# Transferring the compression units past the split, waiting tile by tile in block 1's output, and moving a merge result's evacuation

## The reference

```python
def compress(t, pos_emb, w1, b1, w2):          # once for keys, once for values
    ...
    flat = jnp.moveaxis(blocks, 3, 2).reshape(b, -1, g, CMP_BLOCK * d)
    return jax.nn.gelu(flat @ w1 + b1) @ w2

# block 1
mixed = jnp.concatenate([y_lru, y_moba.astype(x.dtype), y_mem.astype(x.dtype)], axis=-1)
x = x + mixed @ w_out[l]

# block 2
g_conv, g_nsa, g_mem = jnp.split(jax.nn.sigmoid(merge_g), 3, axis=-1)
```

## Time and profile before

| | |
|---|---|
| timed runs | 1745.99, 1747.80, 1747.87 us; median 1747.8 |
| profiled execution | 1752.43 us, span 1750.5 us |
| granted TensorE clock, mean | 0.999 |
| TensorE busy | 1736.1 us (99%) |
| VectorE, ScalarE busy | 61%, 53% |
| moved | 328.51 MB, mean 188 GB/s |

### The profile page before, as it was taken

The page is one execution under the profiler, slowest core; times in us unless marked ns, Lnnn a source line. Parts: engine busy times, 40 slices in busy tenths (PEclk is TensorE's granted clock), DMA queues, the critical chain, the costliest instruction groups (busy, mean ns, idle before and its releaser), DMA issues.

```text
span 1750.5 us, 31143 instructions
## 1 busy us (share of the span) xinstructions
PE 1736.1 (99%) x12548; PEld 1593.0 (91%) x12548; DVE 1073.6 (61%) x1502; ACT 930.8 (53%) x1271; POOL 34.9 (2%) x60
## 2 busy tenths in 40 slices
PE   9999999999999999999999999999999999999998
PEld 9999988999999999988898999899999888989997
DVE  6555787655665566546677555755584557676555
ACT  6444577444454445576756444644464587664443
POOL 0000120000000000000000000000000000000000
PEclk9999999999999999999999999999999999999999
DMA  8655434655665555553355555655554543446552
GB/s 331 235 192 190 170 121 145 219 190 193 223 227 192 190 183 194 182 200 127 139 192 181 193 192 198 231 204 195 192 204 176 191 169 121 168 158 218 190 192 96
DMA packets 47551, 328.51 MB, mean 188 GB/s; under 512 B 5488, under 2 KB 5744, under 8 KB 9072
## 3 DMA queue, kind: packets, MB, share of 16 engines
q1 hardware_dynamic: 44640, 316.86, 50.4%
q10 hardware_dynamic: 2832, 10.54, 1.6%
HBM read 326.33 MB, written 1.05 MB: 187 GB/s over the span
## 4 chain that ended last, share of the span: by engine, by line
PE 94%; ACT 3%; DVE 1%; issue 1%; DMA 0%; POOL 0%; SPq 0%; DVEq 0%; POOLq 0%; ACTq 0%
PE work L1742 19%; PE work L1744 19%; PE work L1743 19%; PE acc L1744 8%; PE acc L1743 8%; PE acc L1742 8%; PE work L1982 4%; PE work L1851 3%; PE acc L2066 1%; PE acc L2048 1%; ACT prob L856 1%; PE acc L2058 1%; ACT hi L662 1%; DMA xT_raw<-xT 0%; PE work L1805 0%
## 5 line engine op out<-in xcount | busy, mean ns | idle before, releaser
L1161 DVE TENSOR_TENSOR lo<-raw,hi 128x2048 fp32r<-128x2048 f32 x271 | 620.3, 2291 | 323.0 <-ACT hi L662 322.8
L662 ACT ACTIVATE hi<-raw 128x2048 fp32r<-128x2048 f32 x271 | 518.7, 1915 | 380.9 <-PE work L1744 354.0
L1742 PE MATMUL work<-xT_hi,hi 128*128 128x256 f32 x2464 | 687.5, 279 | 3.0 <-ACT merge L846 2.5
L1744 PE MATMUL work<-xT_hi,lo 128*128 128x256 f32 x2464 | 683.0, 277 | 0.0
L1743 PE MATMUL work<-xT_lo,hi 128*128 128x256 f32 x2464 | 683.0, 277 | 0.0
L1742 PEld LDWEIGHTS work<-xT_hi,hi 128*128 128x128 f32 x2464 | 463.2, 188 | 12.4 <-issue 6.9
L1743 PEld LDWEIGHTS work<-xT_lo,hi 128*128 128x128 f32 x2464 | 463.8, 188 | 2.3
L1744 PEld LDWEIGHTS work<-xT_hi,lo 128*128 128x128 f32 x2464 | 464.4, 188 | 0.0
L1744 PE MATMUL acc<-hi,hT_lo 128*128 128x512 f32 x480 | 188.8, 393 | 0.0
L1743 PE MATMUL acc<-lo,hT_hi 128*128 128x512 f32 x480 | 188.4, 392 | 0.0
L1742 PE MATMUL acc<-hi,hT_hi 128*128 128x512 f32 x480 | 186.8, 389 | 0.0
(11 more groups left out here) (327 smaller groups left out, 2105.0 us busy)
## 6 DMA issues: line engine op xcount, KB each, us to landing
raw<-stream SPq DMA_DIRECT2D x297, 1024.0 KB, 4.8
mem_in<-mem ACTq DMA_DIRECT2D x3, 1024.0 KB, 5.0
post<-post ACTq DMA_DIRECT2D x6, 512.0 KB, 4.0
memT_raw<-mem2T ACTq DMA_DIRECT2D x2, 1024.0 KB, 7.1
xT_raw<-xT SPq DMA_DIRECT2D x2, 512.0 KB, 5.4
raw<-stream SPq DMA_DIRECT2D x2, 512.0 KB, 6.9
x<-x SPq DMA_DIRECT2D x2, 512.0 KB, 11.0
memT_raw<-mem1T ACTq DMA_DIRECT2D x1, 1024.0 KB, 11.4
```

The costliest lines, as they stand in the source:

```text
L662: nc.scalar.activation(dst, raw[:, s, :], ACT.Copy).then_inc(hi_ready, 1)
L1161: nc.vector.tensor_tensor(lo[:, s, :], raw[:, s, :], hi[:, s, :].bitcast(F32), ALU.subtract).then_inc(lo_ready, 1)
L1742: nc.tensor.matmul(dst, a_hi, b_hi, start=start, stop=False)
L1744: return nc.tensor.matmul(dst, a_lo, b_hi, start=False, stop=stop)
```

## The change

Three edits.

1. A compression unit is transferred by SP straight to its buffer of `whole` (`load_exact`). It waits till TensorE has used the unit three before it, which held that buffer. It has its own two semaphores, `exact_landed`, one for each half of a pair, and `landed` counts these units no more. ScalarE does nothing for it. VectorE counts it in `hi_ready` and `lo_ready` with two `memset`s that wait for nothing. TensorE waits on `exact_landed`. SP's order is: key unit 0, merge 1, key unit 1, value unit 0, value unit 1, then merge 2 and on.
2. `mixed_ready` waits for two attention tiles at kt 4, three at kt 6, four at kt 7; before, for three at kt 4 and four at kt 7.
3. For merge 0 and 1, ScalarE evacuates the result ahead of the split of the merge unit that comes next, where before it did so behind it.

```diff
     def landed(self, n):
-        return 16 * (self.unit(n) // RING + 1)
+        exact = sum(u <= self.unit(n) and u % RING == self.slot(n) for u in EXACT_UNITS)
+        return 16 * (self.unit(n) // RING + 1 - exact)
...
+            def load_exact(n, half):
+
+                sp.wait_ge(unit_used, n - RING + 1)
+                sp.dma_start(whole[:, n % RING, :], stream[n]).then_inc(exact_landed[half], 16)
...
                 base = B1_UNITS + layer * L_UNITS
-                turns = (base + 1 - at) // RING
-                load_turns(at, at + RING * turns)
-                at += RING * turns
+                at = load_turns(at, base + 1)
                 sp.dma_start(params[:, 0:LP_N], l_params[layer]).then_inc(params_loaded, 16)
-            turns = (UNITS - at) // RING
-            load_turns(at, at + RING * turns)
-            for n in range(at + RING * turns, UNITS):
+                first, end = base + L_EXACT[0], base + L_EXACT[-1] + 1
+                at = load_turns(at, first)
+                for n in range(at, first):
+                    load(n)
+                load_exact(first, 0)
+                load(first + 2)
+                load_exact(first + 1, 1)
+                load_exact(first + 3, 0)
+                load_exact(first + 4, 1)
+                at = end
+            at = load_turns(at, UNITS)
+            for n in range(at, UNITS):
                 load(n)
...
             def split_high(sec, n, trip=0):
 
                 s = sec.slot(n)
+                if exact(sec, n):
+                    return
                 wait(act, unit_used, sec.unit(n - RING + 1) + trip * RING)
                 act.wait_ge(landed[s], sec.landed(n) + trip * 16)
-                dst = (whole if exact(sec, n) else hi)[:, s, :]
-                nc.scalar.activation(dst, raw[:, s, :], ACT.Copy).then_inc(hi_ready, 1)
+                nc.scalar.activation(hi[:, s, :], raw[:, s, :], ACT.Copy).then_inc(hi_ready, 1)
...
                     if kind == "merge":
                         split_high(sec, L_MERGE[k] + 2)
+                        merge_out(k)
                         if k < 2:
                             split_high(sec, L_CMP[k] + 2)
-                        merge_out(k)
...
             def split_low(sec, n, trip=0):
                 s = sec.slot(n)
+                if exact(sec, n):
+                    k = 2 * (len(L_EXACT) * sec.layer + L_EXACT.index(n))
+                    nc.vector.memset(passed[:, k:k + 1], 0.0).then_inc(hi_ready, 1)
+                    nc.vector.memset(passed[:, k + 1:k + 2], 0.0).then_inc(lo_ready, 1)
+                    return
                 dve.wait_ge(hi_ready, sec.unit(n + 1) + trip * RING)
-                if exact(sec, n):
-                    k = len(L_EXACT) * sec.layer + L_EXACT.index(n)
-                    nc.vector.memset(passed[:, k:k + 1], 0.0).then_inc(lo_ready, 1)
-                    return
...
                 if kt == LRU_TILES:
+                    pe.wait_ge(tile_lo, jobs[-1].tile - 1)
+                elif kt == KD - 2:
                     pe.wait_ge(tile_lo, jobs[-1].tile)
                 elif kt == KD - 1:
                     pe.wait_ge(tile_lo, jobs[-1].tile + 1)
...
-                        parts_ready(sec, n)
+                        pe.wait_ge(exact_landed[half], 16 * (len(L_CMP) * layer + c + 1))
```

More of the change, by code:

```diff
@@ L81 @@
 UNITS = B1_UNITS + LAYERS * L_UNITS
+EXACT_UNITS = [B1_UNITS + layer * L_UNITS + n for layer in range(LAYERS) for n in L_EXACT]
 F1_MEM, F1_LRU_X, F1_QK, F1_GATE, F1_VC, F1_MEMQ, F1_FILLS = 0, 2, 4, 6, 10, 12, 15
@@ L337, in build @@
         soft = new("soft", [P, 2, 3, TT])
-        passed = new("passed", [P, LAYERS * len(L_EXACT)])
+        passed = new("passed", [P, 2 * LAYERS * len(L_EXACT)])
         lam_t = new("lam_t", [P, 7, LRU_TILES])
@@ L366, in build @@
         landed = [sem(f"landed{s}") for s in range(RING)]
+        exact_landed = [sem(f"exact_landed{half}") for half in range(2)]
         hi_ready, lo_ready, unit_used = sem("hi_ready"), sem("lo_ready"), sem("unit_used")
@@ L571, in load_turns @@
             def load_turns(first, end):
-                with sp.Fori(0, (end - first) // RING) as trip:
+                turns = (end - first) // RING
+                with sp.Fori(0, turns) as trip:
                     for n in range(first, first + RING):
                         load(n, trip)
+                return first + RING * turns
+            def load_exact(n, half):
+                sp.wait_ge(unit_used, n - RING + 1)
+                sp.dma_start(whole[:, n % RING, :], stream[n]).then_inc(exact_landed[half], 16)
             for h in range(2):
```

## The result

| | before | after |
|---|---|---|
| median of the timed runs | 1747.87 us (1745.99 to 1752.07, 15 runs) | 1753.96 us (1751.21 to 1755.55, 15 runs) |
| ratio | | 1.0024, 95% interval 1.0017 to 1.0031 |
| profiled execution | 1752.43 us, span 1750.5 us | 1755.3 us, span 1753.5 us |
| granted TensorE clock, mean | 0.999 | 0.996 |

The change made the kernel slower by 0.24%, 4.2 us by the ratio (3.0 to 5.4), where +2.4 was forecast. The forecast's sign was right and its size short by 1.8 us. The size is not known to the microsecond: the executions of the kernel before spread over 6 us, the two medians lie 6.1 us apart and the means of the same runs, 1748.67 and 1753.43, 4.8. All that follows goes by the ratio.

The account below looks back on a forecast made before the run. TensorE's matmul stream, busy 1736.1 of 1750.5 us, was taken as the bound. Merge 3's delay in two layers less block 1's gain, +1.35 x 2 - 0.3 = +2.4, put the median at 1750.2 us, range 1745.1 to 1753.8.

Parts of the forecast that it names:

- The formula for M3: Merge 3's start in each layer: moves by merge 2's split start, less 773.94, less 0.46; +1.35 us forecast.
- The transfers in layer 0: Both value units and merge 2 issued within 2 us, landing 2.5 us apart; merge 2's split 1.7 us late.
- 1.3 per layer to the rounding: Merge 3's delay from merge 2's late load, taken alike for both layers at 2.5 us spacing of transfers.
- a spacing of 3.8: Upper bound for queued transfers: merge 2 lands at 778.3, shift +3.9 us per layer.
- Rival 2's half-way case: Bunched transfers at 3.1 us each: merge 2 lands at 776.9, +2.5 us per layer, 1752.5 in all; chance 0.07.
- rival 3: Half-clock stretches after gaps before merge 3: 1.7 us each; one more gives 1751.9, one fewer 1748.5; chance upward 0.15.
- Part 3: Evacuation ahead of the next split: merge 1 0.48 us later, 0.46 less behind merge 2's split.
- Rival 1: Merge 2's load not late: -0.36 us per layer, -1.0 in all, 1746.8; chance 0.18.
- Part 2: Block 1's output starts without its 0.41 us wait, may wait 0.1 at kt 7: gain 0.3 (0 to 0.41).
- The sum: Whole kernel: +1.35 x 2 - 0.3 = +2.4 us, median 1750.2, slower by 0.14%.
- the signs to look for: Merge 2's split waits 1.7 us in both layers, landing 7 to 8 us after issue; merge 3 about 1.3 later.
- those that would make it wrong: Merge 2's split right behind merge 1's copy, its landing over 9 us, or half-clock stretches numbering other than one.

Follow-up runs that it names:

- p1_only: The changed kernel with edits 2 and 3 undone, leaving only the direct transfers: 1752.81 us, ratio 1.0022 to the kernel before.
- p23_only: The kernel before with edits 2 and 3 added, without the direct transfers: 1748.78 us, ratio 0.9996 to the kernel before.
- experiments 9 to 11: The changed kernel with 12, 24 or 44 extra products at the very start, one run each: merge 2's last part landed at 12.63 to 14.09 us.
- experiment 7: The changed kernel with value units transferred to the memory of lo and edit 3 for merge 1 alone: 1746.88 us, ratio 0.999 to the kernel before.
- m2_first: The changed kernel with merge 2's load issued ahead of the two value units in SP's queue: 1747.01 us, ratio 0.9984 to the kernel before.
- experiments 5 and 6: 12 unused transposes ahead of merge 3, in the kernel before (1747.13 us, ratio 0.9986) and in the changed kernel (1749.84 us, 1.0006 to the kernel before).
- v_in_lo: The changed kernel with the value units transferred to the memory of lo, issued 8 us earlier: 1747.39 us, ratio 0.9988 to the kernel before.

## Why the prediction came out as it did

**The formula for M3 was right.** It was: M3 moves by the shift of M2's split, less 0.46 for the moved evacuation. Measured, in the order split after, split before, 0.46: 13.17 - 11.27 - 0.46 = 1.44 in layer 0 and 14.38 - 11.27 - 0.46 = 2.65 in layer 1, against 1.44 and 2.66 on TensorE. Without edit 3 (p1_only) the 0.46 falls away, 12.90 - 11.27 = 1.63 against 1.64, and in p23_only 12.24 - 11.27 - 0.46 = 0.51 against 0.48.

**The transfers in layer 0** came as forecast. Issues at 3.07, 3.94 and 5.27 (forecast 3.2, 4.0 and 5.2 from the same origin), landings 2.5 us apart, M2's split 1.4 us late where I had 1.7, M3 +1.44 where I had +1.35. The 358 GB/s per core that the Trainium skill, "DMA: Bandwidth & Descriptors", section Bandwidth, puts on HBM would have made it +2.2; the same section says that this is a core's share when both cores of the domain stream. The trace of this one core lies above it: the first parts of the queued units land 2.48 us apart (the list in experiments 9 to 11), 1.049 MB in 2.48 us or 423 GB/s.

**The term that was mis-sized** is "1.3 per layer to the rounding": layer 1's is 2.66. I had the bound for it, a spacing of 3.8, and set it aside for 2.5, "since it is two transfers really queued together". The 3.8 had another cause. The DMA view of the kernel before, 776 to 777, inside the second transfer of that pair, has the same packet:

```profile
q1 hardware_dynamic: 52, 0.34, 92.4%
q8 instruction: 1, 0.02, 5.8%
```

The 15th part of that transfer landed 2.6 us behind the 15th of the first, which is the distance of the issues, and the sixteenth 1.2 later still. So 3.8 was no rate of a queue. It was one packet, and the right step would have been: 1.35, plus 1.2 to 1.5 in each layer where such a packet falls into the queue ahead of M2's last part. The forecast read M2's landing in layer 0 alone (4.8 us, 1.8 before its split). In layer 1 of the kernel before, a queue 8 transfer starts at 5.69 and M2's load lands 1.1 us later than in layer 0, at 10.56, which its split at 11.27 hides. Its issue and landing time, from the view of the load's line, 1402 to 1404.5:

```profile
L569 SPq DMA_DIRECT2D raw<-stream x1: 333/333/333, 1403.4 to 1403.4; - x1
...
DMA to landing us min/median/max: 5.8/5.8/5.8
```

Which layer meets such a packet was out of the forecast's reach; that one of the two did, and not both or neither, is luck for its total. Rival 2's half-way case (+2.5) had the size of layer 1 nearly right, but not the mechanism: the units do not go slowly one and all.

**The clock, rival 3.** Its rule, one stretch of 3.4 us costs 1.7, is about right: over all traces M3's products took 6.87 to 7.30 us with one stretch and 5.57 to 5.76 without, a difference of 1.1 to 1.7. In the profile two such lengths more are seen in layer 1. On the timed runs the net effect is smaller, 0.1 to 0.7 us and not clear of nothing, since the kernel before pays for its own stretches too. The forecast had counted none.

**Part 3** cost 0.55 at M1 where 0.48 was forecast. At M2 it moves 0.46 from behind the split to ahead of it: a gain while the split waits for its transfer anyway, and about nothing by the forecast's own working (+0.47 before, -0.46 behind) where it doesn't; no run here has M2 on time without it. That the first half is not needed was in the working ("So M1 starts and ends 0.48 later") but not drawn out: experiment 7 takes it back and wins 0.5 us per layer on the trace. Rival 1's -0.36 per layer for an M2 on time was too hopeful as well, it came out at -0.07 and -0.06 in m2_first: the split moved by +0.40 where +0.10 was forecast, 0.07 of it from M1's start and 0.20 because M1's products took 5.6 us and not 5.4 (last section).

**Part 2.** The output's first product waits for nothing (265.21 above). Followed product by product, the stretch from 199 products ahead of it to the first is 0.48 us shorter than before (25.79 against 26.27), and 0.11 of that is given back by the 12th product, so the gain is 0.37. Forecast was 0.3, with a wait of 0.1 at kt 7. The other traces with edit 2 give the same, and those without it none.

**The sum** by its own steps is then 1.44 + 2.66 - 0.37 = +3.7 us of waits on the trace, 3.5 by the timed runs of experiments 5 and 6, and 0.1 to 0.7 for the clock, where the timed ratio has 4.2 (3.0 to 5.4). That 3.5 and 0.7 make exactly 4.2 proves nothing, as both come from the ratios that they are added up to; the waits of the trace and the mean clocks are the independent part. Of the signs to look for, those of the forecast were there, in layer 0 at the forecast size; of those that would make it wrong, the landing of 9.0 in layer 1 and the count of the half-clock stretches were there as well.

The removed copies, 8 of 1.9 us, brought nothing in the changed kernel, because M2's late transfer took their place in front of the split. With M2 on time they are worth 0.55 and 0.73 us: M3 is at 25.09 and 24.91 in v_in_lo and at 25.64 in p23_only, which has the same edits 2 and 3 and keeps the copies.

## What to carry to other kernels

A transfer is not only its own: before an edit lets loads leave earlier, or later, list what stands ahead of the next critical load in the same queue, at 2.5 us for each megabyte as measured here, and issue the critical one first (here three issues in another order made 0.4% between two kernels). When a row seems to show a slow transfer, look at its parts before taking it for a rate. And when a stall is added on the way to TensorE, price the clock behind it too, test that price by filling the gap with idle products, and take it from the granted clocks of many executions: one profile showed 6.8 us of half clock where the timed runs had next to no net change.

## What was not expected of the hardware

**Instruction packets.** The trace has 57 transfers of 16 KB on the instruction queue; outside the loops one comes for every 250 or so records of TensorE and its weight loads taken together, and adding such records at the start moved them. Each takes 0.9 to 1.3 us in most cases (2.1 at most), which is time of one DMA engine of sixteen. With the data queue full, one part in sixteen of each following unit lands 1.1 to 1.5 us behind the 15th until the queue runs dry. Why that is more than the packet's own time, and what else decides when one is asked for, stayed open.

**TensorE's pace at full granted clock varies.** From 100 to 150 us both kernels run the same FFN without a gap, and the windows, of before and then of after, give the same clock but not the same number of products:

```profile
100.00:150.00 50.00, 50.00 (x360) 47.08 (x359) 26.39 (x19) 19.91 (x16) 0.00 (x0) 1.00 0.53 188
...
100.00:150.00 50.00, 50.00 (x365) 46.91 (x364) 27.63 (x19) 20.40 (x15) 0.00 (x0) 1.00 0.54 194
```

The distance between products of 128x256 is 0.118 us in the first and 0.114 in the second. The profiled execution of before ran at the slower pace from about 32 to 200 us and lost 4.1 us in it against the trace of after, most of the 4.6 by which it lay above the median; shorter stretches of it are in all traces. So spans of single profiles must not be compared to the microsecond, and the tables above count from an event next to the stage. The cause stayed open.
